# A transformer block pair on one core: early adaLN blocks in another order, their sixth part summed in the first feed-forward, memory's squares on DVE, and another order around the last merge

## The reference, cut to what matters

```python
mod = silu(c) @ ada_w + ada_b          # 1024 -> 6 x 1024: shift1, scale1, gate1, shift2, scale2, gate2
u = rms_norm(h, norm1_g) * (1 + scale1) + shift1
z = u @ w_in                            # split into q, k, v of two attentions, and two wide gates m_a, m_b
h = h + gate1 * ((sigmoid(m_a) * y_a + sigmoid(m_b) * y_b) @ w_out)
u2 = rms_norm(h, norm2_g) * (1 + scale2) + shift2
h = h + gate2 * (square(relu(u2 @ mlp_w1)) @ mlp_w2)
```

## Time and profile before

| | |
|---|---|
| Median of 3 runs | 1159.46 us (1159.31 to 1161.1) |
| Profiled execution, its own time | 1162.87 us |
| Span of its trace | 1161.1 us |
| PE busy | 1106.9 us (95%) |
| DVE, ACT, POOL busy | 751.0, 590.7, 56.9 us |
| DMA moved | 209.11 MB, 180 GB/s on average |

### The profile page before, as it was taken

One profiled execution on the slowest core, in us unless ns is written; L12 is line 12 of the kernel. 1 busy time (PEld: TensorE's weight loads), 2 busy tenths in 40 slices (PEclk: granted clock), 3 DMA queues, 4 the chain that ended last, 5 costly groups with the idle time before them and its releaser, 6 DMA issues.

```text
span 1161.1 us, 21799 instructions
## 1 busy us (share of the span) xinstructions
PE 1106.9 (95%) x8478; PEld 1062.2 (91%) x8478; DVE 751.0 (65%) x1274; ACT 590.7 (51%) x1041; POOL 56.9 (5%) x86
## 2 busy tenths in 40 slices
PE   4898799999999999999999999998999898999999
PEld 2698698889999999999999998998989888999998
DVE  3657688867489665556666545575766765666643
ACT  2475365655465554444444445696554345444432
POOL 3013110000100000000000000000000000000000
PEclk9899799999999999999999999999999998999999
DMA  9768865145545555555555554434334343555553
GB/s 359 262 233 306 288 238 199 64 142 173 172 169 186 185 185 184 182 177 184 183 182 183 181 182 137 172 128 139 134 110 146 127 146 128 184 183 184 184 184 116
DMA packets 58516, 209.11 MB, mean 180 GB/s; under 512 B 7056, under 2 KB 8592, under 8 KB 57913
## 3 DMA queue, kind: packets, MB, share of 16 engines
q1 hardware_dynamic: 51320, 180.00, 45.1%
q0 software_dynamic: 7104, 27.81, 6.7%
HBM read 204.62 MB, written 3.16 MB: 179 GB/s over the span
## 4 chain that ended last, share of the span: by engine, by line
PE 82%; DVE 7%; ACT 5%; DMA 4%; issue 1%; SPq 0%; DVEq 0%; ACTq 0%
PE bank L632 81%; DMA ada_ring<-in_ada 3%; DVE ring_rounded L1675 2%; DMA wide<-in_ada 2%; DVE ada_acc L1745 2%; ACT rounded_rounded L1265 1%; ACT wide L1447 1%; PE bank L893 1%; DVE part L2197 0%; SPq L584 0%; DVE shared L2217 0%; DVE x L2003 0%; ACT wide_rounded L1314 0%; DVE wide_rounded L1719 0%; DVE shared L2248 0%
## 5 line engine op out<-in xcount | busy, mean ns | idle before, releaser
L1675 DVE TENSOR_TENSOR ring_rounded<-ring,rounded_rounded 128x1024 fp32r<-128x1024 f32 x326 | 398.5, 1227 | 272.1 <-ACT rounded_rounded L1265 263.5
L632 PE MATMUL bank<-u_rounded,rounded_rounded 128*128 128x256 f32 x1528 | 441.7, 290 | 16.3 <-DVE ring_rounded L1675 8.6
L632 PE MATMUL bank<-u_rounded,ring_rounded 128*128 128x256 f32 x1528 | 434.6, 285 | 0.0
L632 PE MATMUL bank<-u_lo_rounded,rounded_rounded 128*128 128x256 f32 x1528 | 433.5, 286 | 0.1
L1265 ACT ACTIVATE rounded_rounded<-ring 128x1024 fp32r<-128x1024 f32 x326 | 342.6, 1054 | 175.7 <-PE bank L632 156.0
L632 PEld LDWEIGHTS bank<-u_rounded,rounded_rounded 128*128 128x128 f32 x1528 | 296.4, 194 | 22.3 <-issue 10.6
L632 PEld LDWEIGHTS bank<-u_lo_rounded,rounded_rounded 128*128 128x128 f32 x1528 | 295.5, 194 | 2.6 <-DVE u_lo_rounded L1721 1.5
L632 PEld LDWEIGHTS bank<-u_rounded,ring_rounded 128*128 128x128 f32 x1528 | 296.6, 194 | 0.0
L632 PE MATMUL bank<-shared_rounded,rounded_rounded 128*128 128x256 f32 x1024 | 259.2, 285 | 0.0
L632 PE MATMUL bank<-wide_rounded,rounded_rounded 128*128 128x256 f32 x832 | 223.4, 284 | 5.8 <-DVE shared_rounded L1976 5.8
L632 PE MATMUL bank<-wide_rounded,ring_rounded 128*128 128x256 f32 x736 | 208.9, 284 | 0.0
(11 more groups left out here) (291 smaller groups left out, 1062.7 us busy)
## 6 DMA issues: line engine op xcount, KB each, us to landing
ring<-in_stream SPq DMA_DIRECT2D x328, 512.0 KB, 3.3
ada_ring<-in_ada POOLq DMA_DIRECT2D x35, 512.0 KB, 5.4
wide<-in_ada SPq DMA_DIRECT2D x6, 512.0 KB, 17.8
shared<-in_ada POOLq DMA_DIRECT2D x4, 512.0 KB, 16.0
mem_parts_kept<-wide_rounded POOLq DMA_DIRECT2D x2, 1024.0 KB, 5.0
shared_rounded<-mem_parts_kept POOLq DMA_DIRECT2D x2, 1024.0 KB, 6.9
x<-in_x_t SPq DMA_DIRECT2D x2, 512.0 KB, 6.5
wide<-in_mem_t SPq DMA_DIRECT2D x2, 512.0 KB, 5.8
```

The lines of the kernel that those rows point to most:

```text
L632: return nc.tensor.matmul(out, lhs, rhs, start=start, stop=stop, skip_group_check=True)
L1675: v.tensor_tensor(R(w), w, R(slot_round(q)), ALU.subtract).then_inc(slot_split, 1)
```

## The change

- The sixteen early ada blocks keep their tiles and their two queues, but are dealt out anew: part 1 (DVE's) mostly from POOL's queue, part 0 (PE's) mostly from SP's, the last block of part 1 last of all. PE sums the squares of x first, then all eight shift blocks, then reduces part 1. DVE takes part 0's diagonals before part 1's columns, and then makes norm and rest of each block of `u` in turn. What reuses the early tiles waits for `scale_summed` too.
- Memory's squares are added by DVE, before qa0 is normalised. `mem_ss` is summed before kb0 and not after kb1, its norm comes after kb1's step, and the list of banks has mem_ss ahead of kb0.
- Of DVE's 32 later ada steps, 15 (before: 18) come ahead of the loop over `h`, 9 (14) in it, and 8 (0), those of part 5, in the first eight m of the first feed-forward. `ada_part(3)` moves from before the loop to h = 2, part 4 from h = 5 to mb0, part 5 from mb0 to after w1_9, with its `ada_reduce` at m = 11, and rope's steps start at m = 12. POOL's queue loads the last five ada blocks, `sg_w` and `sg_ln` after the sums of the first feed-forward's row.
- DVE splits up to su3's reach before it waits for the first head's weights.
- The last two memory heads' products go between the br_b products; br_c goes three, two, two, one ahead of the mix steps; around br_c and mix2 both ACT and DVE handle the new block first and the slots after it. ACT writes `u` of rows 2 and 4 straight from x with the gain as scale; DVE's separate scaling of x is gone.

```diff
+C_BEFORE = ((0, 1, 2), (3, 4), (5, 6), (7,))
...
-ADA_BY_POOL_QUEUE = ((0, 0), (1, 0), (1, 1), (0, 2), (0, 3), (1, 5), (0, 4), (0, 5), (0, 7))
-ADA_BY_SP_QUEUE = ((0, 1), (1, 2), (1, 3), (1, 4), (1, 6), (1, 7), (0, 6))
...
+ADA_BY_POOL_QUEUE = ((1, 0), (1, 1), (1, 3), (1, 4), (1, 5), (0, 3), (1, 6), (0, 6), (0, 7))
+ADA_BY_SP_QUEUE = ((1, 2), (0, 0), (0, 1), (0, 2), (0, 4), (0, 5), (1, 7))
...
-    out += [f"qa{b}" for b in range(4)] + ["kb0", "kb1", "mem_ss", "kb2", "kb3"] + [f"qb{b}" for b in range(4)]
-    out += ["ada2", "cmp_hid_k", "cmp_hid_v", "ada3", "ma0", "cmp_turn_k", "cmp_turn_v"]
...
+    out += [f"qa{b}" for b in range(4)] + ["mem_ss"] + [f"kb{b}" for b in range(4)] + [f"qb{b}" for b in range(4)]
+    out += ["ada2", "cmp_hid_k", "cmp_hid_v", "ma0", "cmp_turn_k", "cmp_turn_v"]
...
+    out += [f"w1_{m}" for m in range(10)] + ["ada5"] + [f"w1_{m}" for m in range(10, KF)]
...
-for part_and_chunk in ADA_BY_SP_QUEUE[:4]:
+for part_and_chunk in ADA_BY_SP_QUEUE[:5]:
...
+sp.wait_ge(scale_summed, KD)
...
-pe.wait_ge(c_spread_ready, 1)
-shift_block(0)
...
-for k in range(1, 5):
+pe.wait_ge(c_spread_ready, 1)
+for k in range(KD):
...
-for k in range(5, KD):
-    shift_block(k)
...
+ps = claim("mem_ss")
+pe.wait_ge(mem_summed, 3)
+done(mm(ps[:, 0:T], mat("ones"), mem_squares[:, 0, :], True, True), "mem_ss")
 for b in range(4):
...
-    if b == 1:
...
-ada_part(3)
...
-    if h == 5:
-        ada_part(4)
+        ada_part(3)
...
-        ada_part(5)
+        ada_part(4)
...
+    if m == 9:
+        ada_part(5)
...
+            if m == 3:
+                values(10)
+            if m == 5:
+                turn(11)
+            if m == 7:
+                values(11)
...
-    if i:
-        values(i - 1)
-    turn(i)
+        if i:
+            values(i - 1)
+        turn(i)
...
-values(11)
...
     claim(f"mix2_{m}")
 for k in range(KD // 2):
-    for m in (2 * k, 2 * k + 1):
+    for m in C_BEFORE[k]:
...
+        pool.wait_ge(scale_summed, KD)
...
-pool.wait_ge(row_squares_ready, (ROW_MEM + 1) * KD)
-for n in (4, 2, 1):
-    ins = pool.tensor_tensor(mem_squares[:, 0:n, :], mem_squares[:, 0:n, :], mem_squares[:, n:2 * n, :], ALU.add)
...
+for n in range(ADA_EARLY + ADA_RING, ADA_BEFORE_STORE):
...
+for n in range(ADA_BEFORE_STORE, ADA_LATE + ADA_RING):
...
-pool.wait_ge(ada_used, ada_steps_through(5))
-pool.dma_start(sg_w[:, :, :], sg_w_d).then_inc(loaded["sg"], 16)
-pool.dma_start(sg_ln[:, :, :], sg_ln_d).then_inc(loaded["sg"], 16)
...
+for n in range(ADA_LATE + ADA_RING, 48):
+    load_ada(n)
+pool.wait_ge(ada_used, ada_steps_through(5))
+pool.dma_start(sg_w[:, :, :], sg_w_d).then_inc(loaded["sg"], 16)
+pool.dma_start(sg_ln[:, :, :], sg_ln_d).then_inc(loaded["sg"], 16)
...
+act.wait_ge(shift_ready, 2)
 for i in range(KD):
     act.wait_ge(u_normed, ROW_X * KD + i + 1)
-    if i % 4 == 0:
-        act.wait_ge(shift_ready, i // 4 + 1)
...
+act.wait_ge(u_normed, (ROW_X + 1) * KD)
+row_inv("mem_ss")
...
-    if b == 1:
...
-        ahead(f"{'up_sb' if before == 0 else 'br_c'}{m}")
+        if before == 0 or m == 0:
+            ahead(f"{'up_sb' if before == 0 else 'br_c'}{m}")
         act.wait_ge(merged_raw, before + m + 1)
         a(R(merged[:, m, :]), lo[:, m, :], ACT.Copy).then_inc(merged_rounded, 1)
+        if before and m < KD - 1:
+            ahead(f"br_c{m + 1}")
...
-def square_and_round(row, last, i):
-    taken(f"{last}{i}")
...
+def round_and_square(row, last, i, gain, after):
+    if after is None:
+        ahead(f"{last}{i}")
+    evacuated(act, f"{last}{i}")
+    a(R(u[:, i, :]), x[:, i, :], ACT.Copy, scale=col(gain, i)).then_inc(u_rounded, 1)
+    if after:
+        ahead(after)
     a(row_squares[:, i, :], x[:, i, :], ACT.Square).then_inc(row_squares_ready, 1)
-    act.wait_ge(u_normed, row * KD + i + 1)
-    a(R(u[:, i, :]), u_lo[:, i, :], ACT.Copy).then_inc(u_rounded, 1)
...
+    round_and_square(ROW_4, "mix2_", i, "ffn2_norm_2", f"mix2_{min(i + 1, KD - 1)}")
...
-ahead("x_ss", 1)
+    if k == KD - 2:
+        ahead("x_ss", 1)
...
+for half in range(2):
+    shift_diagonal(half)
+    at = slice(4 * half, 4 * half + 4)
+    v.tensor_tensor(mod[:, at], mod[:, at], ada_bias(0)[:, at], ALU.add).then_inc(shift_ready, 1)
...
+dve.wait_ge(shift_ready, 2)
...
 for i in range(KD):
     v.scalar_tensor_tensor(out=u_lo[:, i, :], in0=x[:, i, :], scalar=mod[:, 8 + i:9 + i], in1=row_rinv[:, :],
                            op0=ALU.mult, op1=ALU.mult).then_inc(u_normed, 1)
...
+    if i:
+        first_low_part(i - 1)
     if i == 4:
         ahead("x_ss", 2)
...
+first_low_part(KD - 1)
...
+dve.wait_ge(row_squares_ready, (ROW_MEM + 1) * KD)
+for i, n in enumerate((4, 2, 1)):
+    v.tensor_tensor(mem_squares[:, 0:n, :], mem_squares[:, 0:n, :], mem_squares[:, n:2 * n, :], ALU.add).then_inc(mem_summed, 1)
+    dve.wait_ge(mem_summed, i + 1)
...
-for b in range(4):
...
-norm_row(mem_n, mem_n_lo, mem_n, gains("mem_norm_2"), ROW_MEM, None, lambda: ahead("qb0"))
+def between_the_parts():
+    ahead("kb3")
+    ada_step()
+norm_row(mem_n, mem_n_lo, mem_n, gains("mem_norm_2"), ROW_MEM, None, between_the_parts)
...
-    ada_step()
-ada_reduce(3)
-for _ in range(2):
...
-    for _ in range(2 if h < 6 else 1):
...
-    if h == 5:
-        ada_reduce(4)
+    if h == 4:
+        ada_reduce(3)
...
+    if m < KD:
+        ada_step()
...
-    next(steps, None)
+    if m == 11:
+        ada_reduce(5)
+    if m > 11:
+        next(steps, None)
...
+def add_and_split(last, gate, gain, row, reach_later=False):
+    def low_part(i):
+        dve.wait_ge(u_rounded, row * KD + i + 1)
+        v.scalar_tensor_tensor(out=R(u_lo[:, i, :]), in0=x[:, i, :], scalar=gain[:, i:i + 1], in1=R(u[:, i, :]),
+                               op0=ALU.mult, op1=ALU.subtract).then_inc(u_ready, 1)
     for m in range(KD):
-        add_residual(f"{last}{m}", m, gate(m), int(last == "mix2_" and m in (1, 3)))
-        taken(f"{last}{m}")
-        v.tensor_scalar(u_lo[:, m, :], x[:, m, :], gain[:, m:m + 1], None, ALU.mult).then_inc(u_normed, 1)
-        for i in ([m - 1] if m else []) + ([m] if m == KD - 1 else []):
-            dve.wait_ge(u_rounded, row * KD + i + 1)
-            v.tensor_tensor(R(u_lo[:, i, :]), u_lo[:, i, :], R(u[:, i, :]), ALU.subtract).then_inc(u_ready, 1)
+        if not reach_later:
+            ahead(f"{last}{m}")
+        add_residual(f"{last}{m}", m, gate(m), int(last == "mix2_" and m in (1, 3)), False)
+        if m:
+            low_part(m - 1)
+        if reach_later:
+            ahead(f"{last}{m}")
+    evacuated(dve, f"{last}{KD - 1}")
+    low_part(KD - 1)
...
 logits(0)
+ahead("su3")
 attend_scale(0)
...
+            if m == 4:
+                split_output(attn_c[:, 2, :], attn_c_lo2[:, 2, :], "memo2")
+            if m == 7:
+                split_output(attn_c[:, 3, :], attn_c_lo2[:, 3, :], "memo3")
...
+ahead("br_c0")
 for m in range(KD):
-    gate_branch(part[:, m % 2, :], 2 * KD + m, f"br_c{m}")
-    taken(f"br_c{m}")
+    gate_branch(part[:, m % 2, :], 2 * KD + m, f"br_c{m}", False)
+    evacuated(dve, f"br_c{m}")
     v.tensor_tensor(merged_lo2[:, m, :], merged_lo2[:, m, :], part[:, m % 2, :], ALU.add).then_inc(merged_raw, 1)
     if m:
         rest_of_merged(KD + m - 1, m - 1, merged_lo2)
+    ahead(f"br_c{m}")
     dve.wait_ge(merged_raw, KD + m + 1)
 rest_of_merged(2 * KD - 1, KD - 1, merged_lo2)
-add_and_split("mix2_", lambda m: 0.5, gains("ffn2_norm_2"), ROW_4)
```

More of the change, by code:

```diff
@@ L265, in proj_names @@
     out += ["vsw0", "vsw1", "vsb0", "vsb1", "ga", "bias", "kc", "vc", "ks", "kw"]
[L266 to L269 removed]
+    out += [f"qa{b}" for b in range(4)] + ["mem_ss"] + [f"kb{b}" for b in range(4)] + [f"qb{b}" for b in range(4)]
+    out += ["ada2", "cmp_hid_k", "cmp_hid_v", "ma0", "cmp_turn_k", "cmp_turn_v"]
+    out += ["ga_turn", "ma1", "cmp_out_k", "cmp_out_v", "ma2", "ada3", "ma3", "ma4", "ma5", "ma6", "ma7"]
+    out += ["mb0", "ada4"] + [f"mb{b}" for b in range(1, 8)]
     for m in range(KD):
@@ L272, in proj_names @@
     out += [f"mix{m}" for m in range(KD)]
-    out += [f"w1_{m}" for m in range(KF)] + [f"w2_{m}" for m in range(KD)]
+    out += [f"w1_{m}" for m in range(10)] + ["ada5"] + [f"w1_{m}" for m in range(10, KF)]
+    out += [f"w2_{m}" for m in range(KD)]
     def swiglu(p):
@@ L592, in _ @@
             load(0, 0)
-            for part_and_chunk in ADA_BY_SP_QUEUE[4:]:
+            for part_and_chunk in ADA_BY_SP_QUEUE[5:]:
                 load_ada_early(*part_and_chunk)
@@ L738, in sum_gathered @@
                 ps = claim(name)
-                pe.wait_ge(row_gathered, row - ROW_1 + 2)
+                pe.wait_ge(row_gathered, row - ROW_1 + 1)
                 n = gathered_blocks(row)
@@ L1205, in _ @@
             pool.dma_start(mem_parts_kept[1], R(mem_n_lo)).then_inc(mem_stored, 16)
-            for n in range(ADA_OVER_MEM, 48):
+            for n in range(ADA_BEFORE_STORE, ADA_LATE + ADA_RING):
                 load_ada(n)
@@ L1842, in _ @@
                 ada_step()
-            for b in range(4):
```

(18 more changed lines are left out.)

53 lines of the change are left out of this document (14 added, 39 removed).

## The result

The changed kernel takes 1143.79 us (median of 4 runs, 1143.59 to 1145.16) beside 1159.45 for the kernel before: a ratio of 0.9864, 95% interval 0.9847 to 0.9881, so 15.7 us faster. The forecast was 1130 us, with a range of 1121 to 1142. The direction was right; the time lies 1.8 us above the range. The profiled execution took 1143.59 us and its span is 1141.8 us, 19.3 us under the profiled span of before; the medians are 3.6 us closer to each other than that.

The account below looks back on a forecast made before the run. PE, busy 1106.9 of 1161.1 us, was taken as the bound, gains coming from its waits and half clock. Terms summed to -31.3: 1131.6 from the profiled execution, 1128.2 from the median; forecast 1130, range 1121 to 1142.

Parts of the forecast that it names:

- su3: DVE's split ahead of the first head's weights: PE's 3.96 us wait and the half clock after it go, -5.3.
- Last merge and row 4: br_c to the last SwiGLU: new blocks handled before slots shorten the chain and PE's waits, -14 (bounds -16 and -8).
- the merge stays a chain: Rival, last merge: a stall of about 1 us stays for each of six blocks, -8, 1136 us; chance 0.15.
- its two rivals together: Projections stay bound by DMA (0.18) and last merge stays a chain (0.15), both at once: 1143.5 us.
- Three steps fewer before the heads: Projections: PE's two waits (10.8 us) and half clock behind them can go, 16.5, less 3.0 for late landings: -13.5.
- My terms for the early part: Everything forecast ahead of su3, from the start through the first feed-forward: -12 us, 1148.
- My own sign of being wrong: Projections: the forecast is wrong if landings of 8 to 10 us hold DVE there.
- projections stay bound by DMA: Rival, projections: DMA at a share of 0.88 still limits, net there -4, 1137.5 us; chance 0.18.
- ada5 and w1_12: First feed-forward: w1_12 takes ada5's bank, which DVE frees only after w1_11's rest; PE waits 1.4 us.
- The bank order: Projections: mem_ss ahead of kb0 gives kb0 qa2's bank, so it starts later, +2.0 (bounds 0 and +4).
- The start: Early blocks reordered: first product earlier, near 38 to 40 us, -3.0 (bounds -4.5 and -1.0).
- Heads, +1.0: Loop over heads: two DVE steps at h = 6 delay the other attention's first exps, +1.0 (bounds 0 and +2.5).

Follow-up runs that it names:

- the early part: Kernel before with all of the change except the end (su3 split ahead, last merge's order, rows 2 and 4): 1.0029, +3.4 us.
- softplus_first: Changed kernel with DVE's three ada steps ahead of the heads put behind softplus(0): 1139.58 us, ratio 0.9819.
- small_stores: Changed kernel with the two stores of memory's rounded and rest parts cut from 1 MB to 0.13 MB each: 1136.2 us, ratio 0.9793.
- the ada5 fix: Changed kernel with DVE's ada_reduce(5) at m = 10 of the first feed-forward in place of m = 11: ratio 0.9859.
- the three: Changed kernel with ada_reduce(3) at h = 3, the three ada steps behind softplus(0) and ada_reduce(5) at m = 10: 1136.3 us, ratio 0.9799.
- the first measurement: The changed kernel's first timing against the kernel before: 1143.79 us, ratio 0.9864.
- fixes_bank: Changed kernel with ada_reduce(3) at h = 3, three ada steps behind softplus(0), ada_reduce(5) at m = 10, mem_ss between kb1 and kb2 again: 1132.06 us, 0.9751.
- The second profile: Profile from measuring the changed kernel again, with nothing altered: 1146.1 us, ratio 0.9882.
- end_alone: Kernel before with only the last part of the change (su3 split ahead, new order of the last merge and of rows 2 and 4): 0.9835, -19.1 us.
- su3_alone: Kernel before with one line changed, DVE's split of su3's slots ahead of its wait for the first head's weights: 0.9952, -5.6 us.

## Why the prediction missed

**The end was right.** su3: -5.3 forecast, -5.6 measured. Last merge and row 4: -14 forecast, 13.5 left over for it. What ran there is the order that I described, on DVE in the changed kernel (see the earlier trace rows for before):

```profile
921.49 0.41 DVE L2222 SCALAR_TENSOR_TENSOR part<-wide,bank 128x256 f32<-128x256 f32 x1
921.94 0.42 DVE L2277 TENSOR_TENSOR shared<-shared,part 128x256 f32<-128x256 f32 x1
922.28 0.42 DVE L1983 TENSOR_TENSOR shared_rounded<-shared,wide_rounded 128x256 fp32r<-128x256 f32 x1
922.62 1.22 DVE L1674 TENSOR_TENSOR ring_rounded<-ring,rounded_rounded 128x1024 fp32r<-128x1024 f32 x1
```

Gate, add and rest follow each other and the split comes last. The rival that the merge stays a chain is refuted. So it is by chance that the measured 1143.8 us lie next to the 1143.5 that the prediction gave for its two rivals together.

**The step that failed is "Three steps fewer before the heads", -13.5.** It took PE's two waits (10.8 us) and the half clock behind them away, 16.5 us, and put only 3.0 us in their place. From 85 to 160 us PE's waits fell only from 11.7 us (0.94, 4.67, 6.07) to 8.7 (1.23, 1.44, 1.53, 1.28, 3.20), and the stretch of 10.2 us at half clock stayed. Beside it the prediction has no term for ada3's bank, in the heads. My terms for the early part sum to -12.0; it measures +3.4, above even the sum of their worst bounds, +1.0. What the runs show of the 15.4 us between them is this.

- *The wait for the last blocks, about 5 us.* I argued with a mean: 14.1 MB fit in 40 us. But the ring holds three blocks, so the last three can't be asked for before the tenth, eleventh and twelfth of the later steps are done (114 to 117 us), and POOL's queue has two stores just ahead of them, in 14 us in which DMA is full. My own sign of being wrong, landings of 8 to 10 us that hold DVE, came with 11 to 14. Taking three steps away removed PE's own wait for part 3; it left the three steps that stand ahead of softplus(0). I wrote that a part 3 asked for at h = 2 finds DVE "long" past its sixteenth step: true (139.2 us, against PE's reduction at 148.2), but softplus(0), two heads before it, needs DVE too. softplus_first gave 5.2 us, and small_stores showed the stores as 3 to 5 us of the blocks' delay. This is the rival "projections stay bound by DMA", by a named wait and not by the mean rate; ACT's waits for the stream, above, may be a second.
- *ada3's bank, 3.6 us* (2.89 and the half clock behind it). I had worked out this same mechanism for ada5 and w1_12 (forecast 1.4, measured 1.57) and did not apply it to ada3, whose reduction moved to h = 2 on PE and h = 4 on DVE. With the ada5 fix, whose cost was in my sum, the three gave 9.6 (7.5 against the first measurement); without it some 6 to 8 us of unforecast waits.
- *The bank order, +2.0 forecast, 2.4 to 5.6 measured.* kb0 waits, for 1.44 us where I had said 2 to 3.5, but so does kb1 (1.53), which I left out: qa3's norm needs a root whose product PE issues only behind kb0. The third wait on a `qa`, 1.23 us at 87.46, has nothing to do with the bank order: it stands ahead of qa3, for qa0's bank, since DVE's 2.40 us of adds now come before qa0's norm. The prediction has no term for it, it stays with the old bank order (1.22 us at 87.68, fixes_bank), and what it costs no run shows.
- *The start, -3.0.* In the first profile PE ran at half clock from 27.9 to 34.7 us, around the end of a pause of 3.26 us, and the first product came at 41.49, near my lower bound; in the second it did not and the product came at 38.06, my figure for full clock. The second profile ends no earlier for it. In all 13 profiles with the new start this product comes between 38.06 and 41.72, in the five with the old one between 42.35 and 43.15. Undone, the start cost 1.0 to 3.1 us while softplus(0) waits for blocks, and 2.9 us without that wait; that it is swallowed is not shown.
- *The profile that I worked from, about 3.4 us (argued, not shown).* Two more executions with the early code of before reach cq0 at 701.23 and 700.46 us, not at 705.38: end_alone, which differs up to there only in row 2, where PE doesn't wait, and su3_alone, which doesn't differ.

```profile
118.26 0.36 PE L632 MATMUL bank<-u_rounded,rounded_rounded 128*128 128x256 f32 x1 [4.67 <-DVE ring_rounded L1675]
...
114.39 0.36 PE L632 MATMUL bank<-u_rounded,rounded_rounded 128*128 128x256 f32 x1 [1.04 <-DVE ring_rounded L1675]
...
PE bank L632 <- DVE ada_acc L1745: 7.3, 1, 7.3
```

The first row is from before, the other two are from su3_alone. Where the profile had waits of 4.67 and 6.07 us, end_alone has 2.77 and 4.00, and su3_alone 1.04 and 7.30. Both are the fastest executions of their kernels, 2.7 and 3.0 us under the medians, so they overstate the gap; I keep the 3.4 us as its size. I booked the waits as they stood in the one execution, though its time was 3.4 us above the median. What of a wait isn't there in a typical run can't be saved. That a DMA wait varies this much between runs was to be seen in no view of a single one; the gap of 3.4 us was.

The three waits beyond the forecast (7.5 or 9.6, less 1.5), the profile (3.4), the start (0 to 2) and the bank (0.4 to 3.6) make 10 to 17 us, around the 15.4 that were to be explained. The shares may overlap, where what is gained ahead of the blocks is waited for there. Measured in themselves are only the groups that ran as such; the shares of the start, the bank and the profile are point estimates, and how the rest divides stays open.

**Right in the details:** "Heads, +1.0" is matched by the new wait of 1.18 us for the other attention's first weights (1.18 to 1.20 in every profile with the changed early part, in none without). PE went from br_c0 to the first product of the last SwiGLU in 36.2 us (forecast 36 to 37 from values(11), which now stands further ahead). Memory's adds on DVE took 2.40 us (forecast 2.3), and with POOL's adds back the stretched step and split returned as 2.92 and 2.31 us. The five late loads in the feed-forward cost nothing, and PE waits there only for ada5's bank. Row 2's edit shows no wait.

## What to carry to other kernels

A wait for data is removed only if nothing else on the waiting engine needs that data's step to be past: list what stands *behind* the steps that remain, not only who asked for those that went. Don't use a mean bandwidth over 50 us for the last transfers of a stretch; take their own queue: when can each be issued, and how many bytes are ahead of it. And when one small reduction holds a rotating bank, find the taker of that bank for every such reduction that the change moves.

## What was not expected of the hardware

- DMA moved 399 GB/s at a share of 1.01 (118 to 132 us), where I had taken 355 as the ceiling from a share of 0.88. The Trainium skill, Perfetto Trace Analysis, section "Roofline", puts the bound of one active core at about 435 GB/s; the trace stays under it.
- While POOL's adds ran, a DVE step took 2.92 us against 1.28 and a split 2.31 against 1.22, in two kernels alike. The Trainium skill, SBUF — State Buffer, "Who interferes with whom", says that the two engines share a port pair; the runs here agree: the stretch is there when POOL adds and gone when it doesn't.
- The same code gave its first product at 38.06 us with PE at 2.4 GHz throughout the shift blocks and at 41.49 us with 6.8 us at 1.2 GHz, behind pauses of PE of 3.22 and 3.26 us at the same place. A single profile doesn't tell which of the two is usual.
